# The first attention of a two-layer transformer kernel: queries projected and their roots taken ahead of it, the values' compression behind its first scores, its Gelu formed with Tanh

## The chip, the cores and the metric

The kernel runs on one core of a Trainium2 chip. The metric is the device time of one execution in microseconds (us); several executions are run and their median is taken. The engines are TensorE (PE; its weight loads are listed as PEld), VectorE (DVE), ScalarE (ACT), GpSimd (POOL) and SyncE (SP), which here issues the loads of the weights.

## What is computed

The model works on 256 tokens of width 1024. Its first layer is an attention with three kinds of keys (compressed, selected, windowed); a routed mixture of experts, a second attention, another mixture and two dense blocks follow. Only the first attention is touched. The part of it that matters here, cut:

```python
def compress_blocks(k, pos, w1, w2):
    ...
    blk = (k[:, :, idx] + pos).reshape(b, g, n_cmp, CMP_BLOCK * d)
    return jax.nn.gelu(blk @ w1) @ w2

def nsa_attention(xn, w_in, ...):
    q, kc, vc, ks, vs, kw, vw, gl = jnp.split(xn @ w_in, splits, axis=-1)
    q = rms_norm(to_heads(q, N_HEADS), q_gain) * HEAD_DIM ** -0.5
    kc = rms_norm(compress_blocks(to_heads(kc, g), ck_pos, ck_w1, ck_w2), k_gain[0])
    vc = compress_blocks(to_heads(vc, g), cv_pos, cv_w1, cv_w2)
    ...
    p_c = masked_softmax(s_c, dist_c >= 0);  o_c = p_c @ vc
    ...
    o = gc[..., 0:1] * o_c + gc[..., 1:2] * o_s + gc[..., 2:3] * o_w
```

There are 16 heads, 4 groups of keys and values, and 15 compressed keys per group. `jax.nn.gelu` is the form with tanh, x (1 + tanh(sqrt(2/pi) (x + 0.044715 x^3))) / 2.

## The kernel before

Every weight is loaded in chunks of 128 x 2048 floats (1 MB) into a ring of six, by SP, in the order of a plan (`plan_stream`). Chunk n is loaded when chunk n - 6 has been let go. To multiply with full precision, a weight w is split: ACT writes the rounded high part (`wh`, L1222), DVE the rest (`wl`, L1737), each into one of three buffers, and PE makes three products for each block, high by high, low by high, high by low (`mm3`, L454 to L456). Queries and keys are split in the same way after they have been turned: ACT writes the high part of a head (`high`, L1329), DVE the low part (`low`, L1884). Chunks of the kinds "raw" and "ada" are not split: PE (L1031) and DVE (`ada_pieces`, L1982) read them in the ring.

Each engine runs a program written out in order (`tensor_program`, `scalar_program`, `vector_program`); nothing is scheduled. They meet by semaphores: a label such as `("qn", 0)` is raised by one and waited for by another. An engine that waits holds up all that stands behind in its own program. `take()` on ACT and DVE makes the splits that are due at that point.

Ahead of the attention stand, in the program of PE: the projections of keys and values (`kv0` to `kv2`), the compression's first layer for keys (`first_layer(0)`), the turned keys, the queries of heads 0 to 7 (`q0`, 48 products), the second layer for keys (`kc`), the first layer for values (`first_layer(1)`, 32 products, L1031), the turned heads 0 to 7 (`turn_heads`, L612), the turned compressed keys (`kct`, L1054), and the queries of heads 8 to 15 (`q1`, 48 products) with the second layer for values (`vc`, L1063) between its halves. Between `q0` and the turned heads lies a path through the other engines: ACT copies and squares (L1573, L1576), DVE sums the squares (L2279), ACT takes the root, DVE inverts it and multiplies (`q_norm`, L1890, L1893), which raises `("qn", 0)`.

The attention itself takes one head for each step i. PE makes the scores of head i (L624 to L637), then what a table `hooks` gives for that step, then turns the weights of head i - 2 (L647), and multiplies the values of head i - 3 (L659). DVE takes the maxima of step i (L1918), then normalises the weights of step i - 1 (L1923 to L1930), then its own hooks: the compressed scores (L2336 to L2344) at step 0, the low parts of heads 8 to 11 at step 1, the compressed weights (`normalise`, L2350 to L2355, which raises `("pc", 0)`) at step 2. ACT makes the exponentials of step i (L1348), its hooks, and copies of turned weights (L1358). PE's step 3 turns the compressed weights (`turn_compressed(0)`, L1082), which waits for `("pc", 0)`. The rest of the compressed branch, `closing`, waits for `("vb", 1)`, the masked compressed values (L2321).

Of the kernel before, what the change touches and what calls it, by code (L numbers as in the profile page):

```python
# [8 lines left out]
ALU = mybir.AluOpType  # L9
# [112 lines left out]
def plan_stream(w):  # L122
# [42 lines left out]
    plan += compress("a_ck_w1") + w_cols(w_in, 0, 512) + ada("kv", 3) + compress("a_cv_w1") + w_cols(w_in, 512, 512)  # L165
# [44 lines left out]
def program(nc, d, out, plan, first_chunk):  # L210
    with ExitStack() as ctx:
# [204 lines left out]
        def tensor_program(e):  # L416
# [592 lines left out]
            def nsa():  # L1009
# [14 lines left out]
                def first_layer(i):  # L1024
                    chunks = [raw(), raw()]
                    b = bank("fl", i, by=[("gelu", i)])
# [23 lines left out]
                first_layer(1)  # L1050
                turn_heads(("qt", 0), QN[:, :, 0:512], range(8), [("qn", 0)])
                b = bank("kct", by=[("kb",)])
                e.wait_ge(*at("kcn"))
                e.transpose(b[0:64, 0:60], kc, ID[0:60, 0:60]).then_inc(up("full", ("kct",)))  # L1054

                def second_layer():
                    w2 = two(col("w2v", 0, 128))
                    b = bank("vc", by=[("vb", 1)])
# [7 lines left out]
                project("q1", "mix0", lambda t: [("qsq", 1, t)], between=second_layer)  # L1066

                def compressed(hf):
# [7 lines left out]
                    ins.then_inc(up("full", ("cs_full", hf)))  # L1076

# [20 lines left out]
                def late_heads(*js):  # L1098
# [3 lines left out]
                          {0: lambda: compressed(0), 1: lambda: late_heads(0, 1, 2, 3), 3: lambda: late_heads(4, 5, 6, 7), 6: lambda: compressed(1)}, closing,  # L1102
# [110 lines left out]
        def scalar_program(e):  # L1213
# [316 lines left out]
            def nsa():  # L1530
# [31 lines left out]
                def first_layer(i):  # L1562
                    take(2)
                    e.wait_ge(*at("fl", i))
                    e.activation(HTS[i], two(ps("fl", i)[:, 0:120]), ACT.Gelu_apprx_tanh, scale=1.0).then_inc(up("act", ("gelu", i)))

                def q_part(c):
                    if c == 0:
                        take(2)
# [22 lines left out]
                first_layer(1)  # L1592
                e.wait_ge(*at("g8", "aq"))
                high(("qt", 0), range(8), every_other, S[:, 8:9])
                q_part(1)
# [12 lines left out]
                def weigh_and_late():  # L1608
                    late_heads(0, 1, 2, 3)
                    weigh(0)  # L1610

# [117 lines left out]
        def vector_program(e):  # L1729
# [508 lines left out]
            def nsa():  # L2238
# [34 lines left out]
                def q_part(c):  # L2273
                    if c == 0:
                        take(2)
                        ada_pieces(4)
# [90 lines left out]
                def third_hook():  # L2367
                    normalise(0)
# [307 lines left out]
```

## Time and profile before

| | us |
|---|---|
| median of 3 runs | 1260.95 (1259.75 to 1261.28) |
| profiled execution, own time | 1258.35 |
| its span in the trace | 1256.5 |
| PE, DVE, ACT busy | 1197.2, 961.4, 778.5 |

A page of the profile gives busy times of the engines and the costliest groups of instructions; the timeline gives instructions in order with their start from the beginning of the span; "idle before" is time in which an engine stood still, with what released it. The granted clock (PEclk) is 1.00 at 2.4 GHz and 0.50 at 1.2 GHz. The profiled execution's own time is 2.6 us under the median.

### The profile page before, as it was taken

The page shows a single profiled execution, that of the slowest core. Times are in us where ns is not written, and L with a number is a line of the kernel's source. Part 1 is how long each engine was busy: PE and PEld are TensorE (multiplying, and loading weights), DVE is VectorE, ACT ScalarE, POOL GpSimd, SP SyncE. Part 2 cuts the span into 40 slices and gives each one's busy share as a digit, 9 for nine tenths or more (in the row PEclk, how much of TensorE's full clock was granted, in tenths as well). Part 3 has the DMA queues.
Part 4 walks back from the last instruction along what each step waited for, and adds up shares of the span by engine and source line. Part 5 has one row for each costly group of instructions (what it writes and reads, how often), then busy time and mean ns, then how long its engine had stood idle before and what let it go on. Part 6 is the DMA issues. An engine that isn't in the chain of part 4 may idle for free.

```text
span 1256.5 us, 15456 instructions
## 1 busy us (share of the span) xinstructions
PE 1197.2 (95%) x5817; PEld 979.2 (78%) x5817; DVE 961.4 (77%) x1291; ACT 778.5 (62%) x1131; POOL 22.0 (2%) x36
## 2 busy tenths in 40 slices
PE   8998999999998898999999988999998998999997
PEld 7886788888887776888887766887886877888886
DVE  4977858898987886889989777777776866665454
ACT  6566856777777677767777577443446566544433
POOL 0000000000000000000000000000001001000000
PEclk9998999999999999999999999999999999999999
DMA  8750134899995511559999835787776724466520
GB/s 324 298 218 1 68 129 148 316 374 344 359 356 208 227 65 68 210 192 367 371 343 379 321 118 218 279 334 274 285 294 244 287 82 173 179 268 268 175 93 34
DMA packets 41465, 291.83 MB, mean 232 GB/s; under 512 B 4736, under 2 KB 5120, under 8 KB 6576
## 3 DMA queue, kind: packets, MB, share of 16 engines
q1 hardware_dynamic: 40464, 287.82, 60.0%
q0 software_dynamic: 784, 2.63, 0.7%
q8 instruction: 47, 0.77, 0.2%
q10 hardware_dynamic: 144, 0.39, 0.1%
q14 instruction: 26, 0.21, 0.1%
HBM read 289.78 MB, written 1.05 MB: 231 GB/s over the span
## 4 chain that ended last, share of the span: by engine, by line
PE 63%; DVE 19%; ACT 9%; issue 4%; DMA 4%; POOL 0%; DVEq 0%; ACTq 0%; POOLq 0%
PE ps L454 18%; PE ps L456 17%; PE ps L455 17%; DVE wl L1737 6%; DVE AR L1982 4%; ACT wh L1222 4%; DMA ring<-stream_dram 4%; PE ps L659 2%; ACT AR L1348 1%; PE ps L472 1%; ACT XN L1245 1%; PE ps L660 1%; DVE S L1918 1%; ACT XH L1285 1%; DMA AR<-kr_dram 1%
## 5 line engine op out<-in xcount | busy, mean ns | idle before, releaser
L1737 DVE TENSOR_TENSOR wl<-ring,wh 128x2048 fp32r<-128x2048 f32 x228 | 523.6, 2302 | 140.3 <-ACT wh L1222 136.9
L1222 ACT ACTIVATE wh<-ring 128x2048 fp32r<-128x2048 f32 x228 | 436.0, 1915 | 123.3 <-DMA ring<-stream_dram 62.5
L454 PE MATMUL ps<-wh,XH 128*128 128x512 f32 x1040 | 417.6, 402 | 12.7 <-DVE wl L1737 4.1
L456 PE MATMUL ps<-wh,XL 128*128 128x512 f32 x1040 | 406.3, 391 | 0.0
L455 PE MATMUL ps<-wl,XH 128*128 128x512 f32 x1040 | 405.3, 390 | 0.0
L454 PEld LDWEIGHTS ps<-wh,XH 128*128 128x128 f32 x1040 | 195.3, 188 | 61.0 <-issue 9.1
L456 PEld LDWEIGHTS ps<-wh,XL 128*128 128x128 f32 x1040 | 195.2, 188 | 42.4
L455 PEld LDWEIGHTS ps<-wl,XH 128*128 128x128 f32 x1040 | 195.7, 188 | 36.9 <-issue 0.7
L454 PE MATMUL ps<-wh,HT 128*128 128x512 f32 x360 | 141.9, 394 | 4.4 <-DVE HT L2155 2.9
L456 PE MATMUL ps<-wh,HT 128*128 128x512 f32 x360 | 140.5, 390 | 0.0
L455 PE MATMUL ps<-wl,HT 128*128 128x512 f32 x360 | 140.1, 389 | 0.0
L1982 DVE SCALAR_TENSOR_TENSOR AR<-ring,S,AR 128x512 f32<-128x512 f32 x126 | 86.7, 745 | 0.0
L454 PEld LDWEIGHTS ps<-wh,HT 128*128 128x128 f32 x360 | 67.6, 188 | 22.9 <-DVE wl L1737 3.3
L456 PEld LDWEIGHTS ps<-wh,HT 128*128 128x128 f32 x360 | 67.6, 188 | 14.3
L455 PEld LDWEIGHTS ps<-wl,HT 128*128 128x128 f32 x360 | 67.6, 188 | 13.5
L1348 ACT ACTIVATE AR<-ps,S 128x256 f32<-128x256 f32 (+1 forms) x112 | 45.6, 424 | 24.0 <-DVE S L1918 19.5
L1388 ACT ACTIVATE HT<-ps 128x512 fp32r<-128x512 f32 x22 | 13.2, 598 | 67.1 <-PE ps L734 67.1
L1382 ACT ACTIVATE AR<-ps 128x256 f32<-128x256 f32 x44 | 16.7, 384 | 48.9 <-PE ps L456 45.5
L1442 ACT ACTIVATE HT<-ps 128x256 fp32r<-128x256 f32 (+1 forms) x40 | 15.8, 395 | 43.7 <-PE ps L915 43.4
L1918 DVE TENSOR_REDUCE S<-ps 128x2 f32<-128x512 f32 (+1 forms) x56 | 28.8, 552 | 10.7 <-PE ps L637 7.2
L1245 ACT ACTIVATE XN<-H 128x512 f32<-128x512 f32 x40 | 24.9, 624 | 19.1 <-DVE H L1833 12.4
L1452 ACT ACTIVATE AR<-ps,AR 128x256 f32<-128x256 f32 x38 | 18.1, 476 | 24.1 <-PE ps L456 24.1
(309 smaller groups left out, 1238.6 us busy)
## 6 DMA issues: line engine op xcount, KB each, us to landing
ring<-stream_dram SPq DMA_DIRECT2D x272, 1024.0 KB, 5.7
H<-x_dram SPq DMA_DIRECT2D x2, 512.0 KB, 5.0
out_dram<-XN SPq DMA_DIRECT2D x4, 256.0 KB, 2.1
XN<-ag_dram POOLq DMA_DIRECT2D x1, 768.0 KB, 4.6
AR<-pT_dram POOLq DMA_DIRECT2D x2, 256.0 KB, 5.1
AR<-g_final_dram POOLq DMA_DIRECT2D x1, 512.0 KB, 4.8
C<-cols_dram ACTq DMA_DIRECT2D x1, 385.0 KB, 4.7
ring<-stream_dram SPq DMA_DIRECT2D x2, 144.0 KB, 6.2
```

What stands on the lines that cost most here:

```text
L454: e.matmul(o, ah, bh, start=start, stop=False)
L455: e.matmul(o, ah, bl, start=False, stop=False)
L456: return e.matmul(o, al, bh, start=False, stop=stop)
L659: e.matmul(o[b:b + 64, 0:256], v[:, 0, :], pt[:, 0:256], start=not one or u == 0, stop=False, skip_group_check=True)
L1222: e.activation(wh[:, k % WBUF, :], ring[:, n % RING, :], ACT.Copy, scale=1.0).then_inc(up("whi", ("whi", k)))
L1245: e.activation(XN[:, t, half(hf)], H[:, t, half(hf)], ACT.Square, scale=1.0, accum_out=S[:, t + 2 * hf:t + 2 * hf + 1]).then_inc(up("act", ...
L1348: ins = e.activation(o[:, u, :], src[:, u, :], ACT.Exp, scale=1.0, bias=mn[:, t, u:u + 1], accum_out=sm[:, t, u:u + 1])
L1382: e.activation(SG[t], ps("gu", name, j, t)[:, 0:256], ACT.Silu, scale=1.0).then_inc(up("act", ("sg", name, j, t)))
L1452: e.activation(SG[s % 2], ps("gu", name, s)[:, 0:256], ACT.Silu, scale=CWS[:, x, 40:41]).then_inc(up("act", ("sg", name, s)))
L1737: e.tensor_tensor(wl[:, k % WBUF, :], ring[:, n % RING, :], h.bitcast(F32), ALU.subtract).then_inc(up("wlo", ("wlo", k)))
L1918: e.tensor_reduce(mn[:, t, :], two(ps("s", name, i, t)[:, 0:2 * w]), AX, ALU.max, negate=True).then_inc(up("dve", ("mn", name, i, t)))
L1982: ins = e.scalar_tensor_tensor(out=a, in0=v, scalar=c, in1=a, op0=ALU.mult, op1=ALU.add)
```

## The change

In the plan, the two chunks of `q1` now come ahead of the two raw chunks of the values' first layer. PE makes `q1` directly behind `kc`, with the turned heads 0 to 7 and `kct` between its halves; the values' first layer stands in step 0 of the attention, behind the scores of head 0 and the compressed scores, and the second layer in step 2. ACT and DVE split `q1`'s chunks around the turned keys. The Gelu for the values is no longer one ACT instruction: DVE copies the sums and forms the cubic, ACT takes Tanh, and DVE finishes. On DVE this stands at the head of step 1, ahead of the maxima of head 1, and behind the weights of head 0, which are moved ahead too. The second half of what `compressed_keys` did, the masked values, is a function of its own at step 2 (`compressed_values`), ahead of `normalise(0)`. ACT's exponentials of the compressed scores come a step earlier, and two table loads fall away.

```diff
-    plan += compress("a_ck_w1") + w_cols(w_in, 0, 512) + ada("kv", 3) + compress("a_cv_w1") + w_cols(w_in, 512, 512)
+    plan += compress("a_ck_w1") + w_cols(w_in, 0, 512) + ada("kv", 3) + w_cols(w_in, 512, 512) + compress("a_cv_w1")
...
# tensor_program, nsa
-                first_layer(1)
-                turn_heads(("qt", 0), QN[:, :, 0:512], range(8), [("qn", 0)])
-                b = bank("kct", by=[("kb",)])
-                e.wait_ge(*at("kcn"))
-                e.transpose(b[0:64, 0:60], kc, ID[0:60, 0:60]).then_inc(up("full", ("kct",)))
+                def early_heads():
+                    turn_heads(("qt", 0), QN[:, :, 0:512], range(8), [("qn", 0)])
+                    b = bank("kct", by=[("kb",)])
+                    e.wait_ge(*at("kcn"))
+                    e.transpose(b[0:64, 0:60], kc, ID[0:60, 0:60]).then_inc(up("full", ("kct",)))
...
-                project("q1", "mix0", lambda t: [("qsq", 1, t)], between=second_layer)
+                project("q1", "mix0", lambda t: [("qsq", 1, t)], between=early_heads)
...
+                def compressed_and_values():
+                    compressed(0)
+                    first_layer(1, (7,))
...
-                          {0: lambda: compressed(0), 1: lambda: late_heads(0, 1, 2, 3), 3: lambda: late_heads(4, 5, 6, 7), 6: lambda: compressed(1)}, closing,
+                          {0: compressed_and_values, 1: lambda: late_heads(0, 1, 2, 3), 2: second_layer, 3: lambda: late_heads(4, 5, 6, 7),
+                           6: lambda: compressed(1)}, closing,
...
# scalar_program, nsa
-                first_layer(0)
+                take(2)
+                e.wait_ge(*at("fl", 0))
+                e.activation(HTS[0], two(ps("fl", 0)[:, 0:120]), ACT.Gelu_apprx_tanh, scale=1.0).then_inc(up("act", ("gelu", 0)))
+                take()
                 for i in range(2):
                     high(("kt", i), range(4), lambda j, n: KS[0][:, 4 * i + j:4 * i + 4:2, :], col(f"ak{i + 1}"), True)
+                take()
                 q_part(0)
...
-                first_layer(1)
...
+                def weigh_and_bend():
                     weigh(0)
+                    e.wait_ge(*at("cubic"))
+                    e.activation(HTS[0], HTS[0], ACT.Tanh, scale=math.sqrt(2.0 / math.pi)).then_inc(up("act", ("tanh",)))
...
# vector_program, nsa
-                take(2)
+                take(3)
                 for i in range(2):
                     low(("kt", i), range(4), ...)
+                take()
+                ada_pieces(4)
                 q_part(0)
...
+                def gelu():
+                    x, u = two(ps("fl", 1)[:, 0:120]), HTS[0]
+                    e.wait_ge(*at("fl", 1))
+                    e.wait_ge(*at(*then(e.tensor_copy(HTS[1], x), "values")))
+                    e.wait_ge(*at(*then(e.tensor_tensor(u, x, HTS[1], ALU.mult), "gelu", 1)))
+                    e.wait_ge(*at(*then(e.tensor_scalar(u, u, 0.044715, 1.0, ALU.mult, ALU.add), "square")))
+                    e.tensor_tensor(u, u, HTS[1], ALU.mult).then_inc(up("dve", ("cubic",)))
+                    e.wait_ge(*at("tanh"))
+                    e.wait_ge(*at(*then(e.tensor_scalar(u, u, 0.5, 0.5, ALU.mult, ALU.add), "half")))
+                    for j in range(2):
+                        t, v = (w[:, j, :].rearrange(...).broadcast_to([P, 4, 4, 15]) for w in (u, HTS[1]))
+                        ins = e.tensor_tensor(HR[:, j, :, :].rearrange(...), t, v, ALU.mult)
+                    ins.then_inc(up("dve", ("hr",)))
...
# vector_program, attention
                 for i in range(n + 3):
+                    if i == 1 and behind_first:
+                        weights_of(0)
+                        behind_first()
```

**DVE between the split of `q0`'s chunks and `q_norm` of heads 0 to 7.** `wl<-ring,wh` is a split, `KL<-ps,C,HT` the low parts of the keys, `AR<-ring,S,AR` the `ada` pieces, L2279 (now L2286) the sums of squares, `AR<-AR,S` at the end the normalised queries. Before:

```order
L1737 TENSOR_TENSOR wl<-ring,wh 128x2048 x2
L1884 SCALAR_TENSOR_TENSOR KL<-ps,C,HT 64x2x256 x8
L1982 SCALAR_TENSOR_TENSOR AR<-ring,S,AR 128x512 x4
L2279 TENSOR_REDUCE S<-AR 128x8 x2
L1890 RECIPROCAL S<-S 60x1
L2298 TENSOR_SCALAR AR<-AR,S 60x64
L1890 RECIPROCAL S<-S 128x2x8
L1893 TENSOR_TENSOR AR<-AR,S 128x512 x2
L1737 TENSOR_TENSOR wl<-ring,wh 128x2048 x2
```


Now:

```order
L1742 TENSOR_TENSOR wl<-ring,wh 128x2048 x3
L1889 SCALAR_TENSOR_TENSOR KL<-ps,C,HT 64x2x256 x8
L1742 TENSOR_TENSOR wl<-ring,wh 128x2048
L1992 SCALAR_TENSOR_TENSOR AR<-ring,S,AR 128x512 x4
L2286 TENSOR_REDUCE S<-AR 128x8 x2
L1895 RECIPROCAL S<-S 60x1
L2307 TENSOR_SCALAR AR<-AR,S 60x64
L1895 RECIPROCAL S<-S 128x2x8
L1898 TENSOR_TENSOR AR<-AR,S 128x512 x2
```


The two splits of `q1`'s chunks, which stood behind the normalised queries, now stand ahead of the keys' low parts and ahead of the pieces.

**PE around `q1`.** L1048 (now L1049) is `kc`; L1031 (now L1032) the values' first layer; L612 (now L613) turns heads; L1054 (now L1056) is `kct`; the rest are products of `q0` and `q1`. Before:

```order
L456 MATMUL ps<-wh,XL 128x512
L1048 MATMUL ps<-C,S 60x64 x2
L1031 MATMUL ps<-AR,ring 128x60 x32
L612 MATMUL ps<-IDR,AR 128x128 x8
L1054 MATMUL ps<-IDR,AR 64x60
L454 MATMUL ps<-wh,XH 128x512
L455 MATMUL ps<-wl,XH 128x512
```


Now, first behind `kc`, then between the halves of `q1`:

```order
L457 MATMUL ps<-wh,XL 128x512
L1049 MATMUL ps<-C,S 60x64 x2
L455 MATMUL ps<-wh,XH 128x512
L456 MATMUL ps<-wl,XH 128x512
L457 MATMUL ps<-wh,XL 128x512
```


```order
L457 MATMUL ps<-wh,XL 128x512
L613 MATMUL ps<-IDR,AR 128x128 x8
L1056 MATMUL ps<-IDR,AR 64x60
L455 MATMUL ps<-wh,XH 128x512
L456 MATMUL ps<-wl,XH 128x512
L457 MATMUL ps<-wh,XL 128x512
```


The first layer stood between `kc` and the turned heads; now half of `q1` does.

**DVE from the compressed scores of step 0 to the maxima of head 1.** `XN<-XN,S` takes the maximum off the compressed scores; L1918 (now L1939) are the maxima of a head; L1923 to L1930 (now L1915 to L1922) its weights. Before:

```order
L2344 TENSOR_TENSOR XN<-XN,S 128x120 x2
L1918 TENSOR_REDUCE S<-ps 128x2 x2
L1923 RECIPROCAL S<-S 128x4
L1926 TENSOR_TENSOR S<-S 128x4
L1930 TENSOR_TENSOR AR<-AR,S 128x512
L1930 TENSOR_TENSOR AR<-AR,S 128x256
```


Now:

```order
L2366 TENSOR_TENSOR XN<-XN,S 128x120 x2
L1915 RECIPROCAL S<-S 128x4
L1918 TENSOR_TENSOR S<-S 128x4
L1922 TENSOR_TENSOR AR<-AR,S 128x512
L1922 TENSOR_TENSOR AR<-AR,S 128x256
L2317 COPY S<-ps 128x120
L2318 TENSOR_TENSOR S<-ps,S 128x120
L2319 TENSOR_SCALAR S<-S 128x120
L2320 TENSOR_TENSOR S<-S 128x120
L2322 TENSOR_SCALAR S<-S 128x120
L2325 TENSOR_TENSOR AR<-S 128x240 x2
L1939 TENSOR_REDUCE S<-ps 128x2 x2
```


The seven instructions of L2317 to L2325 are new, and the maxima of head 1 stand behind them.

## Rows read from the trace of the kernel before

**Rows 1.** The page, part 1: busy time and share of each engine
```profile
PE 1197.2 (95%) x5817; PEld 979.2 (78%) x5817; DVE 961.4 (77%) x1291; ACT 778.5 (62%) x1131; POOL 22.0 (2%) x36
```

**Rows 2.** Timeline of PE from 70 to 107: start, length, instruction, idle before
```profile
70.08 7.36 PE L1031 MATMUL ps<-AR,ring 128*128 128x60 f32 x64
...
77.27 1.05 PE L612 MATMUL ps<-IDR,AR 128*128 128x128 f32 x8
...
78.42 0.50 PE L454 MATMUL ps<-wh,XH 128*128 128x512 f32 x1
...
83.99 0.95 PE L1063 MATMUL ps<-C,AR 128*120 128x64 f32 x8
...
90.29 0.39 PE L624 MATMUL ps<-HT,XH 128*128 128x512 f32 x1
...
91.80 0.38 PE L624 MATMUL ps<-HT,XH 128*128 128x256 f32 x1 [0.55 <-ACT AR L1576]
...
94.08 0.48 PE L624 MATMUL ps<-HT,XL 128*128 128x512 f32 x1
...
99.37 0.33 PE L647 MATMUL ps<-IDR,AR 128*128 128x128 f32 x1 [2.06 <-DVE AR L1930]
...
106.41 0.45 PE L1082 MATMUL ps<-IDR,XN 128*120 128x128 f32 x2 [0.36 <-DVE XN L2355]
```

**Rows 3.** Timeline of DVE from 56 to 107
```profile
56.09 4.50 DVE L1737 TENSOR_TENSOR wl<-ring,wh 128x2048 fp32r<-128x2048 f32 x2
...
62.13 6.12 DVE L1884 SCALAR_TENSOR_TENSOR KL<-ps,C,HT 64x512 fp32r<-64x512 f32 x8 [1.55 <-ACT HT L1329]
...
68.29 2.74 DVE L1982 SCALAR_TENSOR_TENSOR AR<-ring,S,AR 128x512 f32<-128x512 f32 x4
...
70.94 1.27 DVE L2279 TENSOR_REDUCE S<-AR 128x8 f32<-128x512 f32 x2
...
73.65 1.29 DVE L1893 TENSOR_TENSOR AR<-AR,S 128x512 f32<-128x512 f32 x2
...
84.98 1.29 DVE L2321 TENSOR_TENSOR AR<-ps,C 120x512 f32<-120x512 f32 x2 [0.79 <-PE ps L1063]
...
96.95 1.02 DVE L1918 TENSOR_REDUCE S<-ps 128x2 f32<-128x512 f32 x2
...
100.68 0.74 DVE L1884 SCALAR_TENSOR_TENSOR XH<-ps,S,XH 64x512 fp32r<-64x512 f32 x1 [1.36 <-ACT XL L1329]
...
105.78 0.48 DVE L2355 TENSOR_TENSOR XN<-XN,S 128x120 f32<-128x120 f32 x2
```

**Rows 4.** Windows: length, busy of PE, PEld, DVE, ACT, POOL; PEclk; DMA
```profile
97.30:106.40 9.10, 5.04 (x25) 4.30 (x25) 7.38 (x21) 5.94 (x22) 0.00 (x0) 0.81 0.00 0
...
106.70:110.00 3.30, 3.30 (x11) 2.11 (x10) 1.81 (x7) 3.01 (x11) 0.00 (x0) 0.50 0.00 0
```

**Rows 5.** Timeline of ACT from 59 to 79
```profile
59.34 5.56 ACT L1329 ACTIVATE HT<-ps,C 64x512 fp32r<-64x512 f32 x8
...
73.09 3.69 ACT L1222 ACTIVATE wh<-ring 128x2048 fp32r<-128x2048 f32 x2
...
76.81 1.28 ACT L1565 ACT_TABLE_LOAD   x1
...
78.10 0.27 ACT L1565 ACTIVATE S<-ps 128x120 f32<-128x120 f32 x1
```

**Rows 6.** DMA issues from 53.0 to 53.5: KB each, us to landing
```profile
ring<-stream_dram SPq DMA_DIRECT2D x1, 1024.0 KB, 4.9
```

**Rows 7.** Two DVE forms: group by form (mean ns) and timeline at 43.68
```profile
L2344 DVE TENSOR_TENSOR XN<-XN,S 128x120 f32<-128x120 f32 x2 | 0.5, 282 | 0.0
...
43.68 2.04 DVE L2270 TENSOR_TENSOR AR<-XN,C 128x240 f32<-128x240 f32 x4
```

**Rows 8.** Another idle PE: timeline row, and window of 419 to 423
```profile
418.98 1.14 PE L472 MATMUL ps<-IDR,H 128*128 128x128 f32 x8 [2.58 <-DVE H L2236]
...
419.00:423.00 4.00, 4.00 (x22) 3.48 (x23) 2.13 (x8) 3.30 (x9) 0.00 (x0) 1.00 0.93 387
```

More of the change, by code:

```diff
@@ L1022, in blocks, with first_layer @@
                     ins.then_inc(up("full", ("blk", i)))
-                def first_layer(i):
+                def first_layer(i, of=tuple(range(8))):
                     chunks = [raw(), raw()]
-                    b = bank("fl", i, by=[("gelu", i)])
+                    b = bank("fl", i, by=[("gelu", i)], of=of)
                     e.wait_ge(*at("bl", i))
@@ L1591, in nsa @@
                 root(qss[:, :, 0:8], "qss", 0, 1).then_inc(up("act", ("qroot", 0)))
-                first_layer(1)
                 e.wait_ge(*at("g8", "aq"))
                 high(("qt", 0), range(8), every_other, S[:, 8:9])
+                take(2)
                 q_part(1)
@@ L1901, in q_norm, with attention, weights_of @@
                 ins.then_inc(up("dve", (name, c)))
-            def attention(name, pairs, jo, gated=False, hooks={}, splits=()):
+            def attention(name, pairs, jo, gated=False, hooks={}, splits=(), behind_first=None):
                 n = len(pairs)
                 late = []
+                def weights_of(m):
+                    _, sm, fa = stat(m)
+                    e.wait_ge(*at("ex", name, m, 0))
+                    e.reciprocal(fa, sm).then_inc(up("dve", ("fa", name, m)))
+                    e.wait_ge(*at("fa", name, m))
+                    if gated:
+                        e.tensor_tensor(fa, fa, GT[:, :, 3 * m + 1:3 * m + 3], ALU.mult).then_inc(up("dve", ("fg", name, m)))
+                        e.wait_ge(*at("fg", name, m))
+                    for t in (1, 0):
+                        v = p_of(m, t)
+                        ins = e.tensor_tensor(v, v, fa[:, t, :].unsqueeze(2).broadcast_to([P, 2, 256 if t else 128]), ALU.mult)
+                    ins.then_inc(up("dve", ("p", name, m)))
                 def rest(j):
@@ L2317, in compressed_keys, with compressed_values @@
                     ins.then_inc(up("dve", ("kb",)))
+                def compressed_values():
                     e.wait_ge(*at("vc"))
@@ L2365, in first_hook, with second_hook @@
                     compressed(0)
+                def second_hook():
+                    late_heads(0, 1, 2, 3)
                 def third_hook():
+                    compressed_values()
                     normalise(0)
@@ L2376, in nsa @@
                 attention("nsa", nsa_pairs, 0, True,
-                          {0: first_hook, 1: lambda: late_heads(0, 1, 2, 3), 2: third_hook, 3: fourth_hook,
-                           6: lambda: compressed(1), 7: lambda: normalise(1), 8: lambda: turn_compressed(1)}, (8, 11))
+                          {0: first_hook, 1: second_hook, 2: third_hook, 3: fourth_hook,
+                           6: lambda: compressed(1), 7: lambda: normalise(1), 8: lambda: turn_compressed(1)}, (8, 11), gelu)
             def moba():
```

38 lines of the change are left out of this document (7 added, 31 removed).

## Prediction

> **What bounds the kernel now.** I read the page's engine line first: PE is busy for 95% of the span [rows 1], so work moved about outside PE can only bring what PE waits or loses. Then I read PE's timeline through the change's stretch, 70 to 107, for the "idle before" at the end of a row. The reader should see there that PE works without a break from 70 to 91 (the values' first layer, the turned heads, `q1`), and then, in the fill of the attention, stands still: 0.55 us, 2.06 us, and 0.36 us before the compressed weights are turned at 106.41 [rows 2]. The window over that fill sums it up: of 9.10 us PE is busy for 5.04, so it idles for 4.1, and its granted clock is 0.81 in the mean; in the 3.3 us behind it PE is busy throughout, at 0.50, that is 1.2 GHz [rows 4]. So the fill loses about 4.6 us to idling and, behind it, 1.7 us to the clock.
>
> What sets the fill is not PE. DVE's and ACT's timelines, read from the end of `q1` (90.25, where the scores of head 0 begin) to the end of `normalise(0)` (105.78 + 0.48 = 106.26), show one chain: squares of `q1`, maxima of head 0, normalising of the queries, compressed scores, maxima of head 1 at 96.95, ACT's exponentials and high parts, DVE's low parts at 100.68, maxima of head 2, weights of head 1, `normalise(0)` [rows 2, 3]. It takes 16.0 us, 9.3 of them from the maxima of head 1 on. From 106.41 PE has no wait to speak of up to the end of the attention. The forecast is therefore the shift of that one point, PE's turn of the compressed weights.
>
> **The change: the front, up to the end of `q1`.** PE leaves `kc` at 70.1, as before. Half of `q1` takes 5.5 us (78.42 to 83.99) [rows 2], so PE is at the turned heads at 75.6. They need the normalised queries, and DVE's way to these is now longer. Up to 60.6 DVE splits `q0`'s chunks as before (56.09 + 4.50) [rows 3]. The third split waits for ACT, which begins it where the keys' high parts began, 59.34, and takes half of 3.69, say 1.9 [rows 5]; its chunk has landed by then, since that slot of the plan is issued at 53.3 and lands 4.9 us later [rows 6]. ACT's high parts begin at 61.2, and DVE splits until 63.6. DVE's low parts follow 2.8 us behind ACT's high parts (62.13 against 59.34), so at 64.0, and take 6.1: to 70.1 [rows 3, 5]. Then come the other split, 2.3 (72.4), the pieces, 2.65 (75.0), and the sums of squares, 1.3 (76.3) [rows 3]. ACT's root and DVE's reciprocal I put at 0.8, from 0.3 each for small operations [rows 5, 7] and their hand-overs; the normalising takes 1.3: 78.4, against 74.94 before [rows 3]. PE so waits 2.9 us in the middle of `q1`, a wait that was not there: the first layer for values had covered it.
>
> PE then takes 1.15 for turned heads and `kct` (77.27 to 78.42) and 5.5 for the second half of `q1`: it ends at 85.2 instead of 90.25, 5.0 us earlier. Taken out ahead of it were 7.3 (first layer) and 0.95 (second layer) [rows 2]; 2.9 went to the wait, the rest to rounding and a hand-over.
>
> **The change: from the end of `q1` to the compressed weights.** The scores of head 0 and the compressed scores take 94.08 - 90.29 - 0.55 = 3.2 us, the first layer 7.3 [rows 2], and PE does them without a break: 95.7. (The scores of head 0 now need the bank of `kct`, free when `compressed_keys` is done. DVE's low parts and those four small operations reach 84.9, just ahead of 85.2.) Meanwhile DVE finishes the compressed scores and the weights of head 0 by about 93.7 and waits. All that follows on DVE stands behind the Gelu, whose input comes at 95.7: four operations of 128 x 120 at 0.28 and a gap of 0.03 each, 1.2; a hand-over, Tanh at 0.27 like the Gelu of before [rows 5], a hand-over, 0.5 in all; 0.25; two products of 128 x 240 at 0.51 each [rows 7], 1.0. That is 3.0 us: maxima of head 1 at 98.7, against 96.95. From there the chain is the old one, 9.3, since the weights of head 0, now ahead, had lain beside ACT's exponentials (DVE idles 1.36 at 100.68). But `compressed_values`, 1.3, stood in DVE's idle time at 84.98 and is now in the chain ahead of `normalise(0)` [rows 3]: 109.3, against 106.26.
>
> So the chain behind `q1` grows by 7.9 + 0.1 (16.0 to 24.1), the front gives 5.0: **+3.0 us** at full clock. Bounds: the Gelu's part from 2.4 (operations at 0.2) to 3.8 (at 0.5); the wait at the turned heads from 2.4 to 3.4. Together 2.0 to 4.3.
>
> **The clock.** The 2.06 us of idling ended at 99.37 came just ahead of a stretch at half clock (9.10 us at 0.81 are 3.4 us at 0.50), and so did the idling ahead of 106.7 [rows 2, 4]. But PE idled for 2.58 us before 418.98 and was granted 1.00 in the four microseconds after [rows 8]. A new wait of 2.9 us, the longest of these, I take to bring such a stretch more likely than not. It would lie on the turned heads and the second half of `q1`, where PE sets the end: 3.4 us at half clock cost **+1.7**. The stretch behind the fill (3.3 us at 0.50, worth 1.7) I leave as it is, since PE will idle there more than before: about 9 us instead of 4.6 in all.
>
> The Trainium skill, "TensorE: Matmul & The Clock Gate", Part 1, says that the throttled clock is the default and activity releases it; by that, an idle PE of this length pays again, the sum of +4.7. The trace agrees at 99.37 and not at 418.98.
>
> **What costs or gives nothing.** Two table loads go, 1.28 us each [rows 5]. The one at 76.81 lay while ACT had only the high parts to do, which DVE and PE did not need before 80; the other, behind `q1`, lay beside DVE's sums and maxima. The Trainium skill, "ScalarE: Activation LUTs", "What ACT_TABLE_LOAD costs", puts a switch at about 2.66 us with its drain, and counts exp and tanh as one set. By its figure 5.3 us would go from ACT instead of 2.6. The row does not agree: the Gelu starts at 78.10, 1.29 behind the load's start. ACT's split of the second chunk of `q1` lies before `q0` is done. The loads of two later chunks of the plan wait for the first layer, some 20 us longer, but belong to the expert stage. Should an engine find them late there, a microsecond or two comes on top.
>
> **The likeliest result** is 3.0 + 1.7 = +4.7 us. On the profiled execution that is 1258.35 + 4.7 = 1263.05; the median stands 2.6 above that execution, so 1260.95 + 4.7 = 1265.6. Behind the fill PE is bound by its own work, and nothing gives the shift back.
>
> **The rivals.**
> - *The wait comes, the clock stays* (chance 0.27). For it speaks 418.98. +3.0: 1264.0, at the edge of what can be told from no change; 0.2%, 2.5 us, is what I take for that.
> - *Slower by less, or not at all: the clock behind the fill* (0.17). If PE's idling falls so that the stretch of 106.7 to 110.0 is no more at half clock, 1.7 come back: +1.3 with the clock kept in front, 1262.3. Against it speaks that PE idles more, not less, between 101 and 109.
> - *Faster: the moved first layer fills the holes* (0.08). The change puts 7.3 us of PE's work into a stretch where PE idled for 4.6 and lost 1.7 behind. If the compressed weights were ready no later relative to PE's work, so that those 6.3 us went, and of the new wait only 1.3 were left, the time would be 5.0 lower: 1256. What decides is when the maxima of head 1 begin, 10.6 us ahead of the compressed weights: at 95.7 these come as before, at 90.7 they come 5.0 earlier. PE's own order, scores, compressed scores, first layer, speaks against both: the first layer alone ends at 95.7.
> - *More of the clock* (0.08). With a second stretch at half clock on the first layer or the scores of head 1, +6.4: 1267.4.
>
> The forecast itself has 0.40. Its own range is 1264.3 to 1267. The range for 8 in 10 takes in the kept clock with the low bounds and the second rival: 1261 to 1267.6. Slower by over 0.2%: the forecast, the last rival and a good half of the first, 0.40 + 0.08 + 0.16 = 0.64. Within 0.2%: the rest of the first and the second, 0.11 + 0.17 = 0.28. Faster: 0.08.
>
> **What would show each step.** In the changed profile: PE idle of about 2.9 us before the turned heads (L613), released by DVE's normalising; `q1` ended near 87 (85.2 at full clock); the first layer directly behind the compressed scores; DVE idle for some 2 us ahead of the Gelu's copy; hardly any PE wait at the second layer; PE waits ahead of the late heads, of the turned weights of head 1 and of the compressed weights, the last released near 111 by DVE. The prediction is wrong if the wait at the turned heads is short, if the Gelu's seven operations take far from 3 us, or if the turn of the compressed weights comes before 108.

## The result, and the profile after

| | before | changed |
|---|---|---|
| median | 1260.17 (7 runs, 1258.31 to 1261.28) | 1264.95 (7 runs, 1264.40 to 1266.72) |
| ratio | | 1.0041, 95% interval 1.0030 to 1.0051 |

The change costs about 5 us, some 0.4%. A second set of the same kernel gave 1265.85 (4 runs) and a ratio of 1.0047 (1.0031 to 1.0062). The page of the changed kernel, part 1, shows almost the same work on every engine as before [rows 1], 2 us more on PE and 1 us more on DVE. What was lost is waiting, and products made at the lower clock:

```profile
PE 1199.1 (95%) x5817; PEld 980.6 (78%) x5817; DVE 962.4 (76%) x1296; ACT 776.3 (61%) x1129; POOL 22.0 (2%) x36
```

The timeline of PE through the same stretch of the changed kernel (start, length, instruction, idle before and its releaser), beside [rows 2]:

```profile
78.39 1.09 PE L613 MATMUL ps<-IDR,AR 128*128 128x128 f32 x8 [2.39 <-DVE AR L1898]
...
86.76 0.39 PE L625 MATMUL ps<-HT,XH 128*128 128x512 f32 x1
...
89.73 7.33 PE L1032 MATMUL ps<-AR,ring 128*128 128x60 f32 x64
...
96.88 0.48 PE L625 MATMUL ps<-HT,XL 128*128 128x512 f32 x1
...
107.80 0.45 PE L648 MATMUL ps<-IDR,AR 128*128 128x128 f32 x1 [2.23 <-ACT AR L1365]
...
110.19 0.65 PE L1088 MATMUL ps<-IDR,XN 128*120 128x128 f32 x2 [0.88 <-DVE XN L2377]
```

Four things are to be seen (PE's whole program stands 0.2 us later than in the trace of before when the stretch begins: `kc` starts at 69.88 and at 69.71). At the turned heads PE waits for 2.39 us, in a place where it had no wait. `q1` ends at 86.8 instead of 90.3. The first layer, 7.33 us, stands between the compressed scores and the scores of head 1, without a hole. And the compressed weights are turned at 110.19, where they were at 106.41: 3.8 us later.

The timeline of DVE in the changed kernel, beside [rows 3], shows what sets both points:

```profile
61.44 2.29 DVE L1742 TENSOR_TENSOR wl<-ring,wh 128x2048 fp32r<-128x2048 f32 x1 [0.70 <-ACT wh L1229]
...
64.09 6.12 DVE L1889 SCALAR_TENSOR_TENSOR KL<-ps,C,HT 64x512 fp32r<-64x512 f32 x8 [0.37 <-ACT HT L1336]
...
70.25 2.29 DVE L1742 TENSOR_TENSOR wl<-ring,wh 128x2048 fp32r<-128x2048 f32 x1
...
72.46 2.73 DVE L1992 SCALAR_TENSOR_TENSOR AR<-ring,S,AR 128x512 f32<-128x512 f32 x4
...
75.11 1.27 DVE L2286 TENSOR_REDUCE S<-AR 128x8 f32<-128x512 f32 x2
...
77.04 1.29 DVE L1898 TENSOR_TENSOR AR<-AR,S 128x512 f32<-128x512 f32 x2
...
97.11 0.28 DVE L2317 COPY S<-ps 128x120 f32<-128x120 f32 x1 [2.35 <-PE ps L1032]
...
98.91 0.73 DVE L2325 TENSOR_TENSOR AR<-S 128x240 f32<-128x240 f32 x2
...
99.56 1.02 DVE L1939 TENSOR_REDUCE S<-ps 128x2 f32<-128x512 f32 x2
...
107.23 1.28 DVE L2343 TENSOR_TENSOR AR<-ps,C 120x512 f32<-120x512 f32 x2
...
109.57 0.48 DVE L2377 TENSOR_TENSOR XN<-XN,S 128x120 f32<-128x120 f32 x2
```

From 61.4 to 78.3 DVE hardly idles: two splits and the pieces, work that PE does not wait for yet, stand ahead of the queries that PE waits for. Later it is the other way round: DVE waits 2.35 us for the first layer, and then does the Gelu, the maxima of head 1 and everything behind them in one chain up to 110.05.

The windows of the changed kernel (length; busy time and count of PE, PEld, DVE, ACT, POOL; granted clock; DMA share and GB/s), beside [rows 4]:

```profile
79.80:83.20 3.40, 3.40 (x9) 2.62 (x9) 2.58 (x4) 2.07 (x4) 0.00 (x0) 0.50 1.00 424
83.20:86.60 3.40, 3.40 (x16) 2.79 (x16) 2.21 (x6) 1.27 (x2) 0.00 (x0) 0.99 0.33 140
107.20:114.00 6.80, 5.32 (x17) 3.53 (x18) 5.16 (x16) 4.06 (x14) 0.00 (x0) 0.50 0.00 0
```

Behind the new wait PE works at 1.2 GHz for 3.4 us, 9 products where the next window of that length has 16. So 7 products of 0.23 us, about 1.6 us, are lost there; the second half of `q1` takes 7.18 us (79.58 to 86.76) where it took 5.54 before (84.75 to 90.29). The second half clock, from 107.2 on, lasts 6.8 us, 1.5 of them idle. The kernel before has as much of it, in two pieces: 3.3 us behind the fill [rows 4], and these within it, where the changed kernel is at 1.00:

```profile
99.80:103.20 3.40, 3.40 (x16) 3.11 (x14) 2.47 (x4) 1.58 (x5) 0.00 (x0) 0.50 0.00 0
```

Lining up the same instructions of PE in both traces gives the shift along the program: +0.2 us ahead of the change's stretch, +3.9 behind it, 4.0 to 4.2 up to 768, 5.6 from 773, 6.6 from 872 to the end (in times of the changed kernel). So 3.8 us come from the stretch of the change. Of the rest of this pair of traces, 1.4 us lie at a stretch of half clock (3.4 us from 769.3), and 0.9 at this wait, where the clock is at 1.00:

```profile
872.65 0.66 PE L735 MATMUL ps<-IDR,AR 128*128 128x128 f32 x4 [2.17 <-DVE S L1959]
```

It was 1.22 long in the kernel before. DVE, which ends it, waits for a split of ACT, and ACT for the load of a chunk of weights. Both, half clock and this wait, are taken up with the repeated profiles below.

### The profile page after: what moved, and what is told of

It is laid out like the page before. It is cut to its first block, busy times and chain, and to the rows that moved or that the text cites. A ratio compares the mean times of both kernels' runs of the same rounds, so it can differ in the third digit from the quotient of the medians.

```text
span 1263.1 us, 15459 instructions
## 1 busy us (share of the span) xinstructions
PE 1199.1 (95%) x5817; PEld 980.6 (78%) x5817; DVE 962.4 (76%) x1296; ACT 776.3 (61%) x1129; POOL 22.0 (2%) x36
## 4 chain that ended last, share of the span: by engine, by line
PE 62%; DVE 20%; ACT 9%; issue 4%; DMA 4%; POOL 0%; DVEq 0%; ACTq 0%; POOLq 0%
PE ps L455 17%; PE ps L457 17%; PE ps L456 17%; DVE wl L1742 6%; DVE AR L1992 4%; ACT wh L1229 4%; DMA ring<-stream_dram 4%; PE ps L660 2%; ACT AR L1355 1%; PE ps L473 1%; ACT XN L1252 1%; PE ps L661 1%; DVE S L1939 1%; ACT XH L1292 1%; DMA AR<-kr_dram 1%
## 5 line engine op out<-in xcount | busy, mean ns | idle before, releaser
L1939 DVE TENSOR_REDUCE S<-ps 128x2 f32<-128x512 f32 (+1 forms) x56 | 28.8, 550 | 10.9 <-PE ps L638 7.4
```

Of the source, the lines that this page charges most:

```text
L1939: e.tensor_reduce(mn[:, t, :], two(ps("s", name, i, t)[:, 0:2 * w]), AX, ALU.max, negate=True).then_inc(up("dve", ("mn", name, i, t)))
```

## The experiments

My theory had two parts. First: the wait at the turned heads costs its length and the stretch at half clock behind it, and the Gelu with `compressed_values` lengthens DVE's chain. Second: what the whole run shows beyond that is clock that both kernels lose now and then. The rivals were that the wait itself is hidden (the fill absorbs an earlier `q1`), that ACT's table loads are worth more than the rows say, and that the position of the first layer is what costs. All ratios are to the kernel before on the same chip.

**The wait alone.** The pieces go behind the normalised queries:

```diff
# vector_program, nsa
                 take()
-                ada_pieces(4)
                 q_part(0)
...
                 q_norm("qn", "qroot", 0)
+                ada_pieces(4)
                 take(2)
```

> The changed kernel, with DVE's four ada pieces (2.65 us) moved from ahead of q_part(0) to behind the normalising of queries 0 to 7. Theory 1 (the front's wait is PE's and is made by DVE's longer way): the normalised queries are ready at 75.7, PE reaches the turned heads at 76.0, the wait of 2.39 us before L613 goes to under 0.3, q1 runs at full clock and ends near 82.8 instead of 86.7; all behind it comes 3.5 to 4 us earlier, about +1 us against the kernel before. Rival (the fill is set by DVE's chain alone, and PE's lead at the end of q1 is only turned into idling there): the wait goes, but the turn of the compressed weights stays within 1 us of 110.2, about +4 us against the kernel before.

Measured: 1261.77 (11 runs), ratio 1.0023 (1.0005 to 1.0040), but in two groups: six runs of 1257.55 to 1261.77 and five of 1265.76 to 1268.24. The profile is of the upper group. Its timeline of PE:

```profile
75.81 1.03 PE L613 MATMUL ps<-IDR,AR 128*128 128x128 f32 x8
...
82.72 0.47 PE L625 MATMUL ps<-HT,XH 128*128 128x512 f32 x1
...
85.77 12.77 PE L1032 MATMUL ps<-AR,ring 128*128 128x60 f32 x64
...
111.67 0.65 PE L1088 MATMUL ps<-IDR,XN 128*120 128x128 f32 x2 [1.56 <-DVE XN L2377]
```

The wait is gone and `q1` ends 4.0 us sooner than in the changed kernel. But the same 64 records of the first layer take 12.77 us instead of 7.33, and the turned compressed weights come later than ever. Three windows of this kernel say why:

```profile
83.60:87.00 3.40, 3.40 (x32) 3.39 (x31) 2.94 (x6) 2.62 (x6) 0.00 (x0) 1.00 1.01 429
87.00:90.40 3.40, 3.40 (x18) 3.40 (x18) 3.19 (x13) 1.58 (x8) 0.00 (x0) 0.50 0.10 43
90.40:97.20 6.80, 6.80 (x34) 6.80 (x34) 0.12 (x1) 0.00 (x0) 0.00 (x0) 0.50 0.01 2
```

PE was busy without a break, and was granted half the clock all the same. My theory had the low clock as a consequence of the wait; here it is not, and that part failed. I ran the same kernel a second time.

> The same kernel as pieces_behind once more, for its clock: its times fell into two groups, 1257.6 to 1261.8 and 1265.8 to 1268.2, and its profile (span 1264.4) shows PE busy without a break from 70 to 105 and yet at 0.50 from 87.0 to 100.7, beginning 1.3 us into the values' first layer. Theory 1b (a busy PE loses its clock there in some executions only, by where the chip's clock decisions fall): the two groups come again; a profile of the low group shows 1.00 through the first layer, 7.3 us long instead of 12.8, and a span near 1257. Rival (the two groups have another cause): a profile of the low group shows the half clock too.

Measured: 1260.75 (10 runs), ratio 1.0017 (1.0000 to 1.0035); seven runs up to 1261.65, three from 1264.25 on. This profile is of the lower group, span 1257.3. Its timeline of PE and its windows:

```profile
85.09 7.33 PE L1032 MATMUL ps<-AR,ring 128*128 128x60 f32 x64
...
105.55 0.66 PE L1088 MATMUL ps<-IDR,XN 128*120 128x128 f32 x2 [0.89 <-DVE XN L2377]
```

```profile
83.60:87.00 3.40, 3.40 (x32) 3.40 (x32) 3.33 (x9) 2.94 (x9) 0.00 (x0) 1.00 0.89 373
87.00:90.40 3.40, 3.40 (x33) 3.40 (x32) 2.64 (x10) 0.86 (x5) 0.00 (x0) 1.00 0.02 5
```

The same instructions, full clock, and the turn at 105.55, 36.4 us behind the start of `kc`; the changed kernel needs 40.3, the kernel before 36.7. So without the wait the change is even with the kernel before when the clock holds (the 13 runs of the lower groups have the median 1259.64), and some 6 us worse when it falls. This also says what the 3.8 us of the changed kernel are: the wait and the half clock behind it take all of them, and the rest of the change costs nothing and gains nothing.

Eight of 21 runs lie in the upper groups. Each run's mean granted clock, recorded with its time, goes with the group: 0.985 to 0.991 in these eight, 0.992 to 0.996 in the other thirteen.

The narrow products alone do not bring the low clock. In all four profiles of kernels that have the wait and this order on PE (the changed kernel twice, and two of the variants below) the compressed scores and the first layer stand together in the same way, and both run at 1.00.

**A wait filled with work.** Ten products without a use stand where PE waits; what is computed is unchanged:

```diff
                 def early_heads():
+                    for _ in range(10):
+                        e.matmul(PS[6][:, :], IDR[:, :], XHT[:, 0:512], start=True, stop=True)
                     turn_heads(("qt", 0), ...)
```

> The changed kernel, with ten products of 128x512 without a use ahead of the turned heads on PE (2.2 us at full clock, into a bank that the turned heads overwrite), so that PE is busy through the wait. Theory 1 (the idle PE brings the half clock behind it, 3.4 us at 0.50): the turned heads start at 78.4 as before, but the clock stays at 1.00 up to 86, q1 ends near 85.3 instead of 86.7, the time is 1.4 to 1.7 us lower than the changed kernel's. Rival (the half clock of that stretch came by itself): it is there in this profile too, and the time is that of the changed kernel.

Measured: 1266.99 (6 runs, 1262.75 to 1268.32), ratio 1.0054 (1.0040 to 1.0067). Timeline of PE, then windows:

```profile
76.25 2.49 PE L1054 MATMUL ps<-XH,IDR 128*128 128x512 f32 x10
...
88.56 11.82 PE L1032 MATMUL ps<-AR,ring 128*128 128x60 f32 x64
```

```profile
78.80:85.60 6.80, 6.78 (x34) 5.59 (x35) 4.42 (x9) 4.00 (x6) 0.00 (x0) 1.00 0.88 371
90.80:100.00 9.20, 9.20 (x46) 9.20 (x45) 2.61 (x10) 0.84 (x4) 0.00 (x0) 0.50 0.01 2
```

In place the theory held: PE busy, `q1` at 1.00 throughout, ended at 85.6 instead of 86.8 although `kc` began 0.4 us later. In the time it missed, since the clock then fell in the first layer. Over all profiles of the changed kernel and its variants, the low clock on `q1` is there in four of the five that have the wait and in none of the five that have not (this one, the two above, and two below). So it comes with the idle PE, though not each time; that filling a wait is enough to be faster is refuted.

**Wide products ahead of the first layer.** On the kernel of the first experiment, eight products of 512 columns between the compressed scores and the first layer (`e.matmul(PS[6][:, :], IDR[:, :], XHT[:, 2048:2560], ...)` in `compressed_and_values`), again without a use:

> pieces_behind, with eight products of 128x512 without a use (1.7 us) on PE between the compressed scores (16 products of 30 columns) and the first layer (60 columns). Theory 1b (the clock falls since narrow products of 30 and 60 columns stand together, 1.7 and 7.3 us): with wide ones between, PE keeps 1.00 through the first layer in all executions, the high group is gone, and the median is that of the low group and 1.7, about 1261.5. Rival (the first layer alone, or chance, brings it): the high group stays, and comes 1.7 higher, near 1268.

Measured: 1262.65 (12 runs, 1260.28 to 1265.73), ratio 1.0024 (1.0015 to 1.0033). The timeline of PE:

```profile
86.06 2.11 PE L1083 MATMUL ps<-XH,IDR 128*128 128x512 f32 x8
...
88.01 7.25 PE L1032 MATMUL ps<-AR,ring 128*128 128x60 f32 x64
```

The upper group near 1268 is gone: no run has a mean clock under 0.991. The median sits 3.0 us above that of the lower group, of which the added products are 1.95 (from 86.06 to 88.01); the last microsecond is not explained. This fits the view that a long run of narrow products (30 and 60 columns) on a PE that has not idled is what the clock fell in. It is no proof: one profile, and the products also moved everything by 2 us.

**`compressed_values` behind `normalise(0)`** in `third_hook` of the changed kernel:

> The changed kernel, with compressed_values (1.28 us on DVE) called behind normalise(0) instead of ahead of it. Theory 1 (it lies in the chain that ends at the turn of the compressed weights): that turn comes at 108.9 instead of 110.2, and the time is 1.3 us lower than the changed kernel's. Rival (PE is bound by its own work there, or by the clock): the turn comes earlier, but PE's idle time is then spent elsewhere, and the time is the same.

Measured: 1265.13 (5 runs), ratio 1.0033 (1.0020 to 1.0046). The timeline of PE:

```profile
79.89 1.09 PE L613 MATMUL ps<-IDR,AR 128*128 128x128 f32 x8 [2.42 <-DVE AR L1898]
...
109.00 0.63 PE L1088 MATMUL ps<-IDR,XN 128*120 128x128 f32 x2
...
110.00 1.11 PE L660 MATMUL ps<-AR 128*64 128x256 f32 x2 [0.37 <-DVE AR L2343]
```

The turn comes 37.7 us behind `kc` instead of 40.3. Of these 2.7 us the clock gave 1.6 (this run has the wait of 2.42, but 1.00 on `q1` behind it), so the edit gave about 1.1, near the 1.28 of `compressed_values`. But a small wait on the masked values appears behind it, and the time does not tell this kernel from the changed one. The term in the chain is shown in the trace; its worth in the time is not.

**The Gelu as one ACT instruction again**, in the new place, with its two table loads back; two DVE copies spread the result:

```diff
# scalar_program, weigh_and_bend
-                    e.wait_ge(*at("cubic"))
-                    e.activation(HTS[0], HTS[0], ACT.Tanh, ...).then_inc(up("act", ("tanh",)))
+                    e.wait_ge(*at("fl", 1))
+                    e.activation(HTS[1], two(ps("fl", 1)[:, 0:120]), ACT.Gelu_apprx_tanh, scale=1.0).then_inc(up("act", ("gelu", 1)))
# vector_program, gelu: instead of its seven instructions, for j in range(2)
+                        ins = e.tensor_copy(HR[:, j, :, :]..., HTS[1][:, j, :]...broadcast_to([P, 4, 4, 15]))
```

> The changed kernel, with the Gelu for values as one ACT instruction again (Gelu_apprx_tanh, two table loads come back), and two DVE copies behind it, at the same places of both programs. Theory 1 (length of the way from the first layer's end, 97.0, to the maxima of head 1, 99.6): Gelu 0.3 and copies 0.5 with hand-overs bring the maxima of head 1 to about 98.2, where they wait for the scores; ACT's second table load ends at 98.7 and lies beside them; exponentials of head 1 at 98.9 instead of 100.3; the time is 1.2 to 1.5 us lower than the changed kernel's. Rival (the Tanh form spares ACT 2.6 us where it counts): the time is 1 to 2.6 us higher.

Measured: 1261.67 (12 runs: ten up to 1263.84, two at 1265.84 and 1268.17 with a mean clock of 0.988 and 0.986), ratio 1.0020 (1.0007 to 1.0033): about 3 us under the changed kernel's median. The timeline of ACT and DVE around the first layer's end:

```profile
93.61 1.28 ACT L1615 ACT_TABLE_LOAD   x1
...
96.76 0.27 ACT L1615 ACTIVATE S<-ps 128x120 f32<-128x120 f32 x1 [1.86 <-PE ps L1032]
...
97.05 1.28 ACT L1355 ACT_TABLE_LOAD   x1
```

```profile
97.06 0.48 DVE L2317 COPY AR<-S 128x240 f32<-128x240 f32 x2 [2.65 <-ACT S L1615]
```

The first load is over 1.9 us before its input comes. The second ends at 98.33, while DVE copies and takes maxima; ACT's first exponential of head 1 then starts at 98.36, 0.72 us behind the start of the maxima (97.64), and in the changed kernel, without a load, it is the same 0.72 (99.56 and 100.28). So neither load was on the path, and the maxima of head 1 begin 0.9 us after the first layer's sums instead of 2.5. The Tanh form costs 1.6 us here and saves nothing. In the trace the turn is 38.8 us behind `kc`, 1.5 less than in the changed kernel. That the medians lie 3 apart and not 1.5 goes together with a difference in the clock: its mean is 0.993 over these twelve runs and 0.991 over the changed kernel's first seven. Where that half clock lies, two profiles don't show.

**The first layer later.** Built on the first experiment (no wait): the first layer goes behind the scores of head 2, the second layer ahead of the late heads of step 3, the Gelu to DVE's step 2, and `compressed_values` behind `normalise(0)`. Buffers of two tiles are exchanged so that no data is overwritten.

```diff
# tensor_program: hooks of the attention
-                          {0: compressed_and_values, 1: lambda: late_heads(0, 1, 2, 3), 2: second_layer, 3: lambda: late_heads(4, 5, 6, 7),
+                          {0: lambda: compressed(0), 1: lambda: late_heads(0, 1, 2, 3), 2: lambda: first_layer(1, (7,)), 3: second_and_late,
# scalar_program
-                attention("nsa", nsa_pairs, 0, {0: weigh_and_bend, 1: lambda: late_heads(0, 1, 2, 3), ...
+                attention("nsa", nsa_pairs, 0, {1: late_and_weigh, 2: bend, ...
# vector_program
                 def third_hook():
-                    compressed_values()
+                    gelu()
                     normalise(0)
+                    compressed_values()
...
-                           ... 8: lambda: turn_compressed(1)}, (8, 11), gelu)
+                           ... 8: lambda: turn_compressed(1)}, (8, 11))
```

> pieces_behind, with the values' first layer on PE behind the scores of head 2 instead of ahead of those of head 1, its second layer ahead of the late heads of step 3, DVE's Gelu at step 2 ahead of normalise(0), compressed_values behind it, weights of head 0 and ACT's work at their places of before; the buffers of the squares and of the values' blocks change places, so that no exponential waits for the first layer. Theory 1 (the loss is the maxima of head 1 standing behind the first layer): the turn of the compressed weights comes near 102 instead of 106.4 in the kernel before, PE idles for under 1.5 us in the fill, and the time is 3 to 5 us under the kernel before, about 1256. Rival (DVE with the Gelu ahead of normalise becomes the bound): the turn comes at 105 to 106, no change against the kernel before; with a half clock in the first layer 5 us more.

Measured: 1255.85 (6 runs, 1255.30 to 1258.93), ratio **0.9967 (0.9955 to 0.9979)**, faster than both kernels. Its timeline of PE, the window that in the kernel before held 5.04 us of PE's work at 0.81 [rows 4], and the whole fill:

```profile
90.34 7.25 PE L1032 MATMUL ps<-AR,ring 128*128 128x60 f32 x64
...
100.83 1.02 PE L1065 MATMUL ps<-C,AR 128*120 128x64 f32 x8 [1.30 <-DVE AR L2328]
...
102.78 0.38 PE L1084 MATMUL ps<-IDR,XN 128*120 128x128 f32 x2
```

```profile
97.30:106.40 9.10, 7.49 (x53) 6.20 (x52) 7.69 (x23) 4.24 (x18) 0.00 (x0) 1.00 0.37 131
88.00:110.00 22.00, 19.11 (x147) 16.90 (x145) 18.09 (x49) 11.76 (x44) 0.00 (x0) 1.00 0.19 70
```

The first layer now lies where the scores of head 2 are already made, so DVE and ACT work on heads 1 and 2 beneath it. PE is busy for 2.5 us more of that window at full clock, and the turn stands 31.5 us behind `kc`: 5.2 us sooner than before, 8.8 sooner than in the changed kernel. The clock differs too: the kernel before spends 3.4 us on the way to the turn and 3.3 us behind it at half clock, and this kernel none of either. On the way to the turn PE also waits for DVE in the kernel before, so how much of the gain is clock is not shown.

**The first layer later, the wait kept.** The same, without moving the pieces:

> late_layer without the move of the ada pieces: they stand again ahead of the sums of squares, so that the front of the changed kernel, with its wait on PE, meets the fill of late_layer. Theory 1 (two separate losses that add up: the wait in front with its clock, and the maxima of head 1 behind the first layer): PE waits 2.4 us before L613 as in the changed kernel, the turn of the compressed weights comes 2.5 to 4 us later than in late_layer, near 105, and the time is 2.4 to 4 us over late_layer's, 1258 to 1260, no worse than the kernel before. Rival (in a fill set by DVE's chain the front's wait is hidden): within 1 us of late_layer, 1256.

Measured: 1258.91 (11 runs), ratio 0.9990 (0.9981 to 0.9999). Timeline of PE and one window:

```profile
78.66 1.09 PE L613 MATMUL ps<-IDR,AR 128*128 128x128 f32 x8 [2.40 <-DVE AR L1901]
```

```profile
80.50:83.80 3.30, 3.30 (x9) 2.55 (x8) 2.91 (x4) 1.66 (x3) 0.00 (x0) 0.50 1.01 427
```

The wait and its half clock are back, and the median is 3.1 us higher (4.2 in the traces, 35.8 against 31.5 from `kc` to the turn). So the wait is not hidden by the fill: both losses add. The other step, from the changed kernel to this one, is 6.0 us in the medians (1264.95 to 1258.91) and 4.6 from `kc` to the turn. It belongs to the later first layer together with what moved with it: the Gelu, now at step 2, and `compressed_values`, worth about 1.1 by the run above. What each is worth by itself no run shows. The clock has a part in it too: its mean is 0.995 over these eleven runs and 0.991 in the changed kernel, and the fill has no half clock here.

**Both kernels again**, for the clock far behind the change.

> The changed kernel once more, for the spread of its clock. All theories: 1264 to 1267 and 4 to 6 us over the kernel before. Theory 1: the wait of 2.4 us before L613 is there in each profile, the half clock behind it in some; in a profile without it q1 ends near 85.2 instead of 86.7. Theory 1b: without a half clock on q1 the first layer itself may fall to half clock, as in busy_wait, and the time is then 1267 or more.

> The kernel before once more, for the clock behind the fill. Theory 2 (stretches at half clock near 420, 765, 870 and 950 fall in some executions of every kernel, and the first profile of before had none by chance): this profile, or the next, has one or more of them, each costing 0.9 to 1.8 us, and its span is then over 1257. Rival (the kernel before is free of them, and the change brings them by where it puts what follows): none in either profile.

> The same kernel as before_again, and the same question: theory 2 expects stretches at half clock behind the fill in one of the two profiles and a span over 1257; the rival expects none in either.

Measured for the changed kernel: 1265.85; the wait of 2.38 us and the half clock behind it (78.6 to 82.0) are there again, and low clock from 105.9 to 112.7 and again from 423.3, 764.6 and 952.4 on. For the kernel before, one run each with its profile: 1262.97 and 1261.13, spans 1261.1 and 1259.3. Windows of the first of these:

```profile
420.00:423.30 3.30, 3.30 (x9) 2.58 (x8) 2.16 (x8) 3.30 (x8) 0.00 (x0) 0.50 1.01 425
761.30:768.00 6.70, 5.47 (x17) 4.19 (x17) 2.89 (x9) 5.06 (x11) 0.02 (x1) 0.50 0.59 199
```

The stretches near 420 and 765 are thus in the kernel before too; its first profile had neither [rows 8]. The clock is not all: the wait at the load of weights near 870 is 1.22 long in the first profile, 2.54 and 1.89 in these two, 2.17 and 1.60 in the two of the changed kernel, so it varies by a microsecond whatever the kernel. From the start of `kc` to the turn it takes 36.7 us in all three profiles, and the changed kernel 40.3 and 40.2. The spans average 1259.0 over three profiles of before and 1263.4 over two of the changed kernel, 4.4 apart.

## Why the prediction was right

The forecast was +4.7 us to 1265.6, by a wait with its half clock; measured was 1264.95, +4.8 between the medians (the base had moved too, from 1260.95 over three runs to 1260.17 over seven). By its steps:

- **The front on DVE: right.** Third split at 61.3, low parts at 64.0, second split to 72.4, pieces to 75.0, normalised queries at 78.4 were forecast; 61.44, 64.09, 72.46, 75.11 and 78.3 came. Every duration was within 0.1 us of the row it was taken from.
- **The wait at the turned heads: right, 0.5 too large.** 2.9 forecast, 2.39 measured, which is my lower bound: PE came to the turned heads at 76.0, 0.4 us later than I had put it, and the queries were ready 0.1 sooner. The end of the wait, which is what counts for the time, was thus forecast right: 78.4 and 78.39. Taking the wait away gave back its length and the half clock behind it.
- **The clock in front: right, +1.7 forecast and 1.6 measured.** It came in four of five profiles with this wait, and not in that of the kernel with `normalise(0)` moved. The rival "the wait comes, the clock stays" is therefore something that happens in some executions. What the Trainium skill says in "TensorE: Matmul & The Clock Gate", Part 1, that the clock is released by activity, agrees with these four and with the half clock near 420. It doesn't cover the first layer at 0.50 on a PE that was busy throughout. That an idle time as short as this one pays again was my step from it, and stands on the rows alone.
- **The clock behind the fill, left as it is: right in sum.** Before, 6.7 us in and behind the fill were at 0.50 (99.8 to 103.2, 106.7 to 110.0); now it is 6.8 us (107.2 to 114.0). My sum named only the second piece; the first lay within the fill, which DVE's chain sets.
- **The Gelu: right in kind, 3.0 forecast and 2.5 measured.** The two products of 128 x 240 took 0.73 us together, not 1.0; the row of `128x240` at 43.68 [rows 7], of other tiles, was too dear.
- **The chain from the maxima of head 1: right.** 10.6 forecast, 10.5 measured (99.56 to 110.05).
- **The turn of the compressed weights:** 111.0 forecast with the clock, 110.19 measured. The shift of that point is 3.8 and not 4.7. Of the 0.9 too many, 0.5 are the Gelu; `q1` ended 0.1 sooner than forecast (86.76 against 86.9), scores and first layer took 0.2 less and the chain 0.1 less. The wait's 0.5 is not among them, since its end came when forecast.
- **Nothing gives the shift back: right.** PE's program stays at +3.9 to +4.2 from there to 768. So late chunks of the expert stage cost no more than 0.2 us.
- **Table loads for nothing: right, shown by the run with the loads back.**
- **What made up the missing microsecond.** The median moved by 4.8 to 5.2 where the trace's stretch moved by 3.8. Half clock near 420, 765 and 870 to 950, and the wait at the load near 870, cost both kernels in some executions. The mean clocks of the runs say that the changed kernel meets the half clock more often: 0.990 in the four runs of its second set (0.989 to 0.992), 0.9935 in fifteen runs of the kernel before on the same chip (0.990 to 0.995). By these means some 9 us more are at half clock, an estimate, of which 3.4 lie behind the wait. Where the others lie, how much of them falls on a busy PE and what brings them, the profiles don't tell. My forecast had no term for them; that its total fits the median better than its own terms do is luck.

Of the rivals, "the moved first layer fills the holes" was rightly judged by its condition: the maxima of head 1 began at 99.56, behind the 95.7 at which it would have broken even. The run with the first layer two scores later bears the condition out in direction: its maxima of head 1 begin 19.2 us behind the start of `kc` (90.47 and 71.24), against 27.2 before, and the turn comes 5.2 us sooner after `kc` (3.7 us in the median). It does not bear out the size. My rule of 10.6 us from these maxima to the compressed weights would have made 8.0 us earlier into 6.7; in that kernel the Gelu stands in the chain behind them instead, and it takes 11.8 (90.47 to 102.22). That the gain came near my 5.0 is chance. "More of the clock" did not come in the stretch of the changed kernel, but is what happened in some executions once its wait was removed.

## What to carry to other kernels

Work that is moved to fill a hole has to stand behind the scores that the other engines will work on during it; placed ahead of them it pushes the whole chain. Ahead of the scores of head 1, moving 7.3 us of work gained nothing even without the wait in front (36.4 us from `kc` to the turn, 36.7 before); two scores later, with the Gelu and the masked values moved along, it gained 5.2. On the engine that feeds a wait, look at what stands ahead of the awaited result and is not yet needed: 2.7 us of pieces were worth 4 us at the end of `q1` and 3 in the median, 1.6 of them through the clock. Filling such a wait with products of no use did not help. One profile of a kernel is one draw of its clock: compare the start-to-start time over the stretch in question, in more than one profile, before a shift of a microsecond or two is put down to an edit.

## What the hardware showed that I had not expected

- A PE without any idle time was granted 0.50. In the first layer, behind other narrow products, it lost the clock for 13.7 us (87.0 to 100.7), and the 64 records took 12.77 us instead of 7.33. The same program a second time kept 1.00. The run times lie in two groups some 6 us apart, and the mean clock is 0.985 to 0.991 in the upper and 0.992 to 0.996 in the lower. Why the clock falls there stays open: with the wait ahead of `q1`, the same narrow products kept 1.00 in four profiles of four.
- The same idle time doesn't always cost the clock: 2.4 us did in four of five profiles, and 2.58 us ahead of 418.98 did not in the first profile of the kernel before, while that place is at 0.50 in its other two.
- Small DVE instructions with a broadcast operand were cheaper here than the nearest rows of this kernel suggested: 0.37 us for each of the two 128 x 240 products, where 0.51 is the mean of four of that size on other tiles [rows 7].
